# Output weights and the first convolution block loaded during the last attention steps, and the attention chunks first in the output product

## What is computed

```
def merge(conv_y, gc, attn_o, ga, w_out):
    mix = jnp.concatenate([conv_y * jax.nn.silu(gc), attn_o * jax.nn.silu(ga)], axis=-1)
    return mix @ w_out

xp = xp + merge(cy, gc, o, ga, w_out[l])
y_prompt = rmsnorm(xp, final_norm_g)[:, N_META:]
```

## Time and profile before

| what | us |
|---|---|
| median of 3 runs (lowest to highest) | 1630.58 (1630.3 to 1631.38) |
| the profiled execution's own time | 1629.15 |
| its span, first to last instruction | 1627.5 |
| TensorE busy, VectorE busy | 1452.4, 1009.3 |
| ScalarE busy, POOL busy | 681.3, 417.5 |
| mean granted clock of TensorE, of full speed | 0.962 |

### The profile page before, as it was taken

One profiled execution on the slowest core, in us unless ns is written; L12 is line 12 of the kernel. 1 busy time (PEld: TensorE's weight loads), 2 busy tenths in 40 slices (PEclk: granted clock), 3 DMA queues, 4 the chain that ended last, 5 costly groups with the idle time before them and its releaser, 6 DMA issues. The chain is left out here.

```text
span 1627.5 us, 27734 instructions
## 1 busy us (share of the span) xinstructions
PE 1452.4 (89%) x10518; PEld 1273.5 (78%) x10518; DVE 1009.3 (62%) x2122; ACT 681.3 (42%) x1108; POOL 417.5 (26%) x270
## 2 busy tenths in 40 slices
PE   5688988998998978999979999999999987389998
PEld 4686888996998967999948888877777766268886
DVE  3342898888989868889844445546676655343322
ACT  4444512235211235223123565556566656354331
POOL 2112223450221840331221110111322433053220
PEclk9998998999999989999987999999999999789999
DMA  7742166230337550322467055221112122485542
GB/s 228 235 125 53 35 109 136 59 101 5 94 97 270 120 144 1 104 55 81 122 180 161 25 120 119 52 70 36 41 48 91 58 75 79 124 212 163 165 155 97
DMA packets 183353, 172.69 MB, mean 106 GB/s; under 512 B 58956, under 2 KB 155348, under 8 KB 182700
## 3 DMA queue, kind: packets, MB, share of 16 engines
q1 hardware_dynamic: 176572, 152.91, 35.2%
q10 hardware_dynamic: 6136, 16.95, 3.5%
q0 software_dynamic: 512, 1.05, 0.2%
HBM read 109.35 MB, written 58.19 MB: 103 GB/s over the span
## 5 line engine op out<-in xcount | busy, mean ns | idle before, releaser
L845 PE MATMUL psum<-xh,wh 128*128 128x384 f32 (+1 forms) x1040 | 346.0, 333 | 24.1 <-ACT hst L782 11.7
L845 PE MATMUL psum<-xh,wl 128*128 128x384 f32 (+1 forms) x1040 | 342.6, 329 | 0.0
L845 PE MATMUL psum<-xl,wh 128*128 128x384 f32 (+1 forms) x1040 | 342.4, 329 | 0.0
L1447 ACT ACTIVATE pts<-psT 128x768 f32<-128x768 f32 (+3 forms) x172 | 150.4, 875 | 212.4 <-PE psT L1732 190.3
L1620 DVE CUSTOM_DVE_ANT_0 L<-psU,mask 128x512 f32<-128x512 f32 (+3 forms) x260 | 148.2, 594 | 120.0 <-PE psU L1722 111.8
L845 PEld LDWEIGHTS psum<-xh,wh 128*128 128x128 f32 x1040 | 198.4, 191 | 27.5 <-ACT hst L782 12.4
L845 PEld LDWEIGHTS psum<-xl,wh 128*128 128x128 f32 x1040 | 198.3, 191 | 0.0
L845 PEld LDWEIGHTS psum<-xh,wl 128*128 128x128 f32 x1040 | 198.0, 190 | 0.0
L693 POOL TENSOR_TENSOR wl<-uw,wh 128x1024 fp32r<-128x1024 f32 x44 | 121.8, 2769 | 277.2 <-ACT wh L730 277.2
L995 DVE TENSOR_SCALAR_CACHE_REDUCE hit<-scores,T 128x1792 bf16<-128x1792 f32 (+8 forms) x120 | 184.6, 1539 | 11.7 <-issue 0.9
L1748 PE MATMUL psO<-pts,vs 128*64 128x128 f32 x2176 | 154.6, 282 | 19.0 <-ACT pts L1447 18.2
(11 more groups left out here) (268 smaller groups left out, 2406.9 us busy)
## 6 DMA issues: line engine op xcount, KB each, us to landing
uw<-in_w_in SPq DMA_DIRECT2D x28, 512.0 KB
uw<-in_w_in SPq DMA_DIRECT2D x32, 256.0 KB
qt<-d_q SPq DMA_DIRECT2D x16, 512.0 KB, 4.2
xst<-in_x_prompt SPq DMA_DIRECT2D x15, 512.0 KB, 4.1
xr<-in_x_prompt SPq DMA_DIRECT2D x15, 512.0 KB, 4.4
out_y_prompt<-fin SPq DMA_DIRECT2D x15, 512.0 KB, 3.0
gate<-d_ga SPq DMA_DIRECT2D x17, 256.0 KB, 4.5
d_mix<-mix SPq DMA_DIRECT2D x17, 256.0 KB, 2.2
```

What stands on the lines that cost most here:

```text
L845: last = nc.tensor.matmul(u[:, 0:k * P], a[:, w % 2, cc, :], x[:, s0:s0 + k, cc, :], start=(cc == 0 and e == 0), stop=(cc == KC - 1 and e ...
L1447: A.activation(out, src, ACT.Copy).then_inc(act_pt, 1)
```

## The change

One buffer `big` is allocated for the whole program and takes the places of several others: `scores`, `sq`, `gb`, `sig` and `run` in the early stages, `yc` and `rx` in the attention. Its first 8192 columns hold the output weights afterwards, the next 1024 the first block (`y0`, `gc0`, the last tile's). SyncE issues these loads in the attention, one piece a step from step 49 on, and the first block at step 57. In `mix_out` all low parts of weights and both low parts of the first tile are VectorE's; POOL starts with the second tile. ScalarE's and VectorE's queues for the first tile are written out anew, and the chunks' order is 4, 5, 6, 7, 0, 1, 2, 3. The core of the diff:

```diff
+            def load_output_weights(x):
+                wo = output_weights(mem)
+                if x < 4:
+                    c, side = 2 * (x // 2), x % 2
+                    r = C + 256 * side + 64 * c
+                    sp.dma_start(wo[64 * side:64 * side + 64, CC + c:CC + c + 2, :],
+                                 t.w_out[0, r:r + 128, :].rearrange("(c p) n -> p c n", p=64)).then_inc(mem.wo_in[x // 2], 16)
+                else:
+                    q = x - 4
+                    sp.dma_start(wo[QA * q:QA * q + QA, 0:CC, :],
+                                 t.w_out[0, P * q:P * q + P, :].rearrange("(c p) n -> p c n", p=QA)).then_inc(mem.wo_in[2], 16)
...
+                x = p - TURN_STEP[-1] - 2
+                if x == 0:
+                    sp.wait_ge(pe_pt, pt_no["Y", len(NORM) - 1, NORM[-1][-1]] + 1)
+                if 0 <= x < 4 + NQ:
+                    load_output_weights(x)
+                if x == 4 + NQ:
+                    load_first_block()
...
-W_ORDER = [c for pair in zip(range(CC, KC), range(CC)) for c in pair]
+W_ORDER = list(range(CC, KC)) + list(range(CC))
...
-            load_block(0)
-            for c in range(CC):
-                for q in range(NQ):
-                    r = P * q + QA * c
-                    sp.dma_start(wst[QA * q:QA * q + QA, c, :], t.w_out[0, r:r + QA, :]).then_inc(w_ld[c], 16)
-                if c == 0:
-                    load_am(0)
-                    load_x(0)
+            load_am(0)
+            load_x(0)
             load_block(1)
...
+                if k == 0:
+                    w_high(CC)
+                    w_high(CC + 1)
+                    act.wait_ge(a_in[0], 16)
+                    A.activation(fh[:, 0, CC:KC], am[:, 0], ACT.Copy).then_inc(am_hi0, 1)
+                    w_high(CC + 2)
+                    w_high(CC + 3)
+                    act.wait_ge(mem.head_in, 16 * (1 + NQ))
+                    for c in range(CC):
+                        last = A.activation(y0[:, c, :], y0[:, c, :], ACT.Silu, bias=lb[:, c:c + 1], scale=lg[:, c:c + 1])
+                    last.then_inc(swish_in, 1)
+                    w_high(0)
+                    act.wait_ge(block_done, 1)
+                    A.activation(fh[:, 0, 0:CC], gc0[:, :, :], ACT.Copy).then_inc(gc_hi0, 1)
+                    for c in range(1, CC):
+                        w_high(c)
+                    continue
...
+                if k == 0:
+                    w_low(CC)
+                    dve.wait_ge(am_hi0, 1)
+                    TT(fl[:, 0, CC:KC], am[:, 0], fh[:, 0, CC:KC].bitcast(f32), ALU.subtract).then_inc(am_lo0, 1)
+                    for c in range(CC + 1, KC):
+                        w_low(c)
+                    dve.wait_ge(swish_in, 1)
+                    TT(gc0[:, :, :], y0[:, :, :], gc0[:, :, :], ALU.mult).then_inc(block_done, 1)
+                    dve.wait_ge(gc_hi0, 1)
+                    TT(fl[:, 0, 0:CC], gc0[:, :, :], fh[:, 0, 0:CC].bitcast(f32), ALU.subtract).then_inc(gc_lo0, 1)
+                    for c in range(CC):
+                        w_low(c)
+                    continue
```

More of the change, by code:

```diff
@@ L517, in project_and_select @@
         hit = sb("hit", [128, LP], bf16)
-        run = sb("run", [128, LP])
+        run = mem.big[:, SCOLS:SCOLS + LP]
         iqpad = sb("iqpad", [64, NS * NS * IH])
@@ L1124, with output_weights, first_block @@
 TURN_STEP = [s + 5 for s in SUM_STEP]
+def output_weights(mem):
+    return mem.big[:, 0:KC * D].rearrange("p (c n) -> p c n", n=D)
+def first_block(mem):
+    at = KC * D
+    return [mem.big[:, at + x * CC * P:at + (x + 1) * CC * P].rearrange("p (c t) -> p c t", t=P) for x in range(2)]
 def attend_and_convolve(nc, t, mem):
@@ L1351, in _, with load_first_block @@
                              t.conv_b[0].rearrange("(q g a) -> g q a", g=4, a=QA)[g:g + 1].to_broadcast([WIN, NQ, QA])).then_inc(fc_in, 16)
+            def load_output_weights(x):
[9 more added lines that the diff above has]
+                                 t.w_out[0, P * q:P * q + P, :].rearrange("(c p) n -> p c n", p=QA)).then_inc(mem.wo_in[2], 16)
+            def load_first_block():
+                y0, gc0 = first_block(mem)
+                tok = slice(LAST * P, NT * P)
+                sp.wait_ge(cT_out[0], 16)
+                sp.dma_start(y0, t.d_y[:, :, tok].rearrange("c p t -> p c t")).then_inc(mem.head_in, 16)
+                for q in range(NQ):
+                    sp.dma_start(gc0[QA * q:QA * q + QA], t.d_gc[q, :, tok].rearrange("(g a) t -> a g t", a=QA)).then_inc(mem.head_in, 16)
             for p in range(NP_ + 3):
@@ L1883, in mix_out @@
             ("swish_in", "block_done", "hi_done", "lo_done", "pe_o", "res_done", "sq_done3", "rstd_done3", "fin_done")]
-        w_ld = [sem(f"wo_ld{c}") for c in range(CC)]
-        w_hi, conv_lo, attn_lo = sem("wo_hi"), sem("wo_conv_lo"), sem("wo_attn_lo")
+        w_hi, w_lo = sem("wo_hi"), sem("wo_lo")
+        am_hi0, am_lo0, gc_hi0, gc_lo0 = sem("am_hi0"), sem("am_lo0"), sem("gc_hi0"), sem("gc_lo0")
         gf_in = sem("gf_in")
@@ L1912, in load_block @@
                 w = len(tiles) * P
-                if k >= 2:
-                    sp.wait_ge(lo_done, sum(len(b) for b in BLOCKS[:k - 1]))
+                if k >= 3:
+                    sp.wait_ge(lo_done, sum(len(b) for b in BLOCKS[1:k - 1]))
                 sp.dma_start(y[:, k % 2, :, 0:w], t.d_y[:, :, tok].rearrange("c p t -> p c t")).then_inc(y_in[k % 2], 16)
@@ L1989, in _ @@
                 if what == "tile":
-                    if n == 1:
-                        for c in range(CC + 1, KC):
-                            attention_low(c)
+                    if n == 0:
+                        n += 1
+                        continue
                     b, e = block_of[k]
                     s = n % FS
-                    pool.wait_ge(hi_done, n + 1)
+                    pool.wait_ge(hi_done, n)
                     G.tensor_tensor(out=fl[:, s, 0:CC], in0=gc[:, b % 2, :, e * P:(e + 1) * P], in1=fh[:, s, 0:CC].bitcast(f32), op=ALU.subtract)
@@ L2004, in w_high @@
             def w_high(c):
-                act.wait_ge(w_ld[c % CC], 16 * (NQ + 2))
+                if c >= CC:
+                    act.wait_ge(mem.wo_in[(c - CC) // 2], 32)
+                else:
+                    act.wait_ge(mem.wo_in[2], 16 * NQ)
                 A.activation(wh[:, c, :], wst[:, c, :], ACT.Copy).then_inc(w_hi, 1)
-            for c in range(CC, KC):
-                for side in range(2):
-                    r = C + 64 * (c - CC) + 256 * side
-                    act.dma_start(wst[64 * side:64 * side + 64, c, :], t.w_out[0, r:r + 64, :]).then_inc(w_ld[c % CC], 16)
             act.wait_ge(eps_set, 1)
@@ L2091, in _ @@
                 TT(gc[:, k % 2, :, 0:w], y[:, k % 2, :, 0:w], gc[:, k % 2, :, 0:w], ALU.mult).then_inc(block_done, 1)
-                if k == 0:
-                    for c in range(CC):
-                        conv_low(c)
             finish(NT - 1)
@@ L2154, in build @@
         sb = lambda n, s, d=f32: ctx.enter_context(nc.sbuf_tensor(n, s, d))
+        big = sb("big", [128, SCOLS + LP + 9 * P])
+        wo_in = [ctx.enter_context(nc.semaphore(f"wo_in{s}")) for s in range(3)]
+        head_in = ctx.enter_context(nc.semaphore("head_in"))
         cst = sb("cst", [128, NCONST])
```

60 lines of the change are left out of this document (29 added, 31 removed).

## The result

The changed kernel took 1614.12 us (median of 4 runs, 1606.44 to 1620.11) beside 1630.98 us of the kernel before (4 runs taken between them). The ratio is **0.9884, 95% interval 0.9857 to 0.9911**, 18.9 us less with an interval from 14.5 to 23.3 us (the ratio is not that of the two medians, which lie 16.9 us apart). On the median of 1630.58 that is 1611.7 us. The sign was right; the forecast of 1617.1 was too small a gain, and its range, which ended at 1613.6, missed the time by 1.9 us.

A forecast was written before the change was run, and what follows sets the result against it. TensorE bounds the steady output stage and the second tile's start sets the end; from the 1630.58 us median, -15.2 (earlier start) + 1.7 (clock) = -13.5 gives 1617.1 us, range 1613.6 to 1621.

The forecast's parts named there:

- The bound and the mechanism: Output stage: TensorE bounds the steady part, the second tile's start sets the end; early loads make that start earlier.
- "15.2 us" for the new start: Output stage's start: second tile begins at 1430.0 instead of 1445.17, a gain of 15.2 us.
- The size of a low part, 1.2: Output stage's start: each low part of a weight takes VectorE 1.2 us, since POOL is idle then.
- The rival of 3.07: Output stage's start: low parts stay at 3.07 us on VectorE alone; gain 3.1, time 1627.5, chance 0.05.
- "+1.7" for the clock: Between first two tiles: TensorE's longer idle brings one 3.4 us stretch at half clock, costing 1.7 us; bounds 0 and 3.4.
- eight of nine upstream idles: Past 100 us: of nine idles of 2.2 to 3.8 us, eight had a half-clock stretch just after; basis for the clock term.
- Attention "at nothing": Attention: early loads fit into free transfer share and cost nothing; up to 1.5 us allowed.
- The 2 us of slack: Attention: the last group of early loads drains about 1386, 2 us before the next queries' load is issued at 1387.88.
- The third block "at nothing": Before tile four: the third block lands about 1438.5, some 2.5 us of slack, no term; a slower drain gives up to 2 us.
- The tail, taken as fixed: From the second tile's start to the end: 182.3 us follow, whatever comes before.
- The no-stretch rival, 1615.4: Between first two tiles: the clock stays full over the idle, no half-clock stretch; 1615.4 us, chance 0.25.

The follow-up runs named there:

- e4: Changed kernel with the first block's load moved back to the output stage's start, the weights still loaded early; ratio 0.9900.
- e8: Changed kernel with POOL's first subtraction for the second tile repeated once or twice, lengthening TensorE's idle to 3.91 or 5.25 us; ratios 0.9902 and 0.9912.
- e6: Changed kernel with the weights and first block loads issued at the output stage's start instead of in the attention; ratio 0.9993.
- e1: The changed kernel run once more without any edit; 1612.78 us, ratio 0.9892.
- e3: Changed kernel with the low parts of the four convolution weights made by POOL instead of VectorE; ratio 0.9902.
- e9: Changed kernel with the second tile's attention half rounded and subtracted (by POOL) while VectorE still makes the weights' low parts; ratio 0.9888.
- e7: Changed kernel with all early loads issued in one step, ahead of the last tile's queries, instead of spread over groups; ratio 0.9971.
- e2: Kernel before with only the shared buffer taken over, loads and orders untouched; ratio 0.9974.
- e11: Kernel before with only the shared buffer, measured a second time on another occasion; ratio 0.9987.
- e10: Kernel before with a group of logits matmuls near 872 us repeated, lengthening that stretch by 5.0 us; ratio 1.0013.

## Why the prediction was right, and where it was wrong

The forecast was a gain of 13.5 us, and the range ended at 1613.6; 1611.7 lies below it. The mechanism held. Two terms of the sum were mis-sized, the start's 15.2 us and the clock's 1.7, and one was missing.

**The bound and the mechanism: right.** The second tile's start set the end, in every kernel, but for the half-clock stretches behind it in e4 and e8. The gain is that of the early loads (e6, without them, takes it away whole), the chain of the new start ran through the steps as they were listed, VectorE was the later engine, and from its product of the second block to the second tile it was 5.04 us again. The first tile lay inside (e1's longer half-clock stretch there only shortened the idle behind it, 1.75 instead of 2.58 us, and moved nothing).

**"15.2 us" for the new start: 16.8, a mis-sized term.** Of the 1.6 us, 1.0 is the landing of the first attention chunk. I took 3.6 us, the median of all 17 such loads, most of which share the transfer system with others; alone at the head of the queue it took 2.59. The rest is small: four low parts 4.54 us instead of 4.8, one fh and its low part closer together.

**The size of a low part, 1.2: right.** 1.22 alone, 1.16 apart in a row; e3 and e9 measure the other end. The rival of 3.07 is out.

**"+1.7" for the clock: the step that failed.** In the profiled run it is 0, in e4 1.6, in e8 1.3 and 2.6. The mechanism was right and the size was off. The prediction had an idle of 3.2 us; it was 2.6, and at this length no stretch followed in two of three profiled executions at this place. I had carried eight of nine upstream idles over to this one. Near 1157 they hold: twelve of the thirteen profiled executions that idled 2.5 to 2.6 us there had a stretch. Why the tile boundary differs is open.

**Attention "at nothing": nearly right.** About 0.8 us. The wait of TensorE's weights load for the queries was 0 to 0.34 us in the four kernels without the early loads and 0.17 to 0.60 in the eight with them. The 2 us of slack that the prediction saw were not there: the last group landed by 1391.2, when the queries' load was just being issued (1391.09). e7 shows what more of it costs.

**The third block "at nothing": right.** Its last load landed 27.5 us after the stage's start, where 29.9 were foretold, and tile four started on time.

**The tail, taken as fixed:** 0.57 us shorter, with the early loads and without (e6), not with the buffer alone (e2, e11). It lies behind the last VectorE instruction, in the last store. The four kernels with the longer tail (before, e2, e11, e10) are those in which ScalarE still issues eight loads of weights in the stage; whether that is the cause was not tested.

**What no term had: about 2 us.** By the ledger the changed kernel gains 16.8 + 0.57 - 0.8 = 16.6 us, a better sum than the forecast's 13.5 by 1.6 (start), 1.7 (clock) and 0.6 (tail), less 0.8. Measured were 18.9 and, again, 17.6. Made in the same way for the eleven kernels with the shared buffer other than e7, the measured gain is larger than the ledger's every time, by 1.0 to 3.8 us, 2.1 on average. Those that share a group share its runs of before, and all share one profile of it, so this is not eleven proofs; e2 and e11, two groups, say 3.8 and 1.7. For the changed kernel alone the 2.3 us lie inside the interval of its gain. The prediction counted the buffer only as a place for the loads and gave it no term and no bound. That was an omission, though a small one. Where these 2 us arise is open: the profiled executions differ by more than that among themselves upstream, in the waits for xl and in half-clock stretches.

So the miss of 5.4 us is 3.3 us of mis-sized terms (start and clock) and some 2 us that come with the buffer; the tail and the attention's 0.8 nearly cancel. The no-stretch rival, 1615.4, had the clock right; with the true start it would have been 1613.8.

## What to carry to other kernels

Where a stage begins with a full transfer system and idle engines, find a place earlier in the same queue where its share is low, and spread the loads there in groups that drain before the next load that an engine waits for; the same loads in one group gave 14 of 18 us back. Take a transfer's time to landing from a row in the same circumstances (first in an empty queue, or among others), not from the median of its kind. And write down a term with a bound for everything that a change touches, a new place in memory too, also when its likeliest value is nothing.

## What was not expected of the hardware

- At the same place of the program an idle of about 2.5 us was followed by 3.4 us at half clock in some executions and not in others (near 1157: behind 2.50 us in e11, not behind 2.62 in e2; near 1240: behind 2.62 in after, not behind 2.46 in e11; at the tile boundary: behind 2.55 in e4, not behind 2.58 in after). Behind 3.91 and 5.25 us it came. One stretch cost 1.3 to 1.6 us.
- Issues behind many large transfers took longer themselves: four that take 2.75 us took 9.09 in e7, and a load behind them landed after 10.9 us instead of 4.1.
- A delay of 5.0 us put in ahead of 880 us cost 2.1 us of time (interval from 0.8 less to 5.1 more). In the profiled execution TensorE was 9.1 us late, and 7.1 of them were made good between 1150 and 1260.
- POOL and VectorE on the same subtraction of 128x1024: VectorE 1.22 us alone, up to 2.33 with one POOL instruction of 1.3 us beside it and up to 3.43 with POOL at the same work. A product of 128x1024 that began behind a POOL product of 128x2048 took 5.12 us, and ended 1.1 us behind it.
